# A decoder step on one core: first in-projection tiles ahead of the norm, tokens loaded in halves, the gate chain moved, and squares and splits interleaved at the key entry

## The chip, the cores and the metric

The kernel runs on one core of one Trainium2 chip. The metric is the device time of one execution in microseconds (us), as the median of several runs. PE is TensorE (matmuls), DVE is VectorE, ACT is ScalarE, POOL is GpSimd, and SP is the engine that here only issues transfers.

## The reference

One step of a small decoder with two layers, for 512 prompt tokens and 8 samples of 8 tokens each, together 576 token columns with 1024 features:

```
h = x
h += gdn_mixer(rmsnorm(h))        # h @ w_in -> causal conv of 4 taps -> silu -> q, k, v;
                                  # gates b, a -> beta, g; chunked gated delta rule; @ w_out
h += conv_ffn(rmsnorm(h))         # up, conv of 3 taps, silu, gate, down
k, v = rope(rmsnorm(h) @ w_kv)    # shared keys and values, computed once
h += diff_attention(rmsnorm(h), [paged cache, k], [paged cache, v])
h += conv_ffn(rmsnorm(h))
y = rmsnorm(h) * final_norm
```

All is float32. The outputs are y, the new recurrent state, the last rows before each convolution, and the new keys and values.

## The kernel before, in words

Features lie on the 128 partitions and tokens along the row: `hT` holds 8 blocks (m or k, 0 to 7) of 128 features by 576 tokens. A float32 product is made from three reduced-precision ones (`mm3`, L695): each operand is split into a high part (made by ACT: `high` for tokens, `weights` for weights) and a low part, the rest (made by DVE for tokens: `low`; by POOL for weights: its own `low`, or a line of its own in loops). The norm's factor per token is not multiplied into the tokens; it is multiplied into the product later (`rb`, a row of 576 factors; `rt`, the same by tokens), so products can begin before the norm is known.

The order of each engine's work is written out by hand: five programs run side by side and wait on semaphores. Loads go through SP's and ACT's queues.

**Entry.** PE turns the tokens from `X` into `hT` block by block (L680 to L686), with small transposes of the gains (L676) ahead and of the convolution rows (L691) in between. DVE evacuates a block (L1345) and makes the low part of the one before (L1347). ACT makes the high part and the squares of each block (L1921, L1922) and, before blocks 2 and 3, splits the two first weight tiles (L1919). POOL adds up the squares (L2346) and makes the low weights (L2345). Then PE computes the 16 gate columns (L806), the sums for the norm (L811), and the loop over the 32 in-projection tiles (`channels3`, L818 to L830). A tile is 128 output features: 48 matmuls of 288 columns (two token halves, eight blocks, three products). Two pairs of PSUM banks and two weight slots alternate, so tile t+2 waits for the evacuation of tile t and for the split of its weights.

**Tile loop.** For tiles 0 to 23 DVE multiplies by `rb` into a padded buffer (`pads`) and runs the four taps (L1396 to L1418). ACT then applies silu and, for the query and key tiles 0 to 15, squares the result (L1948 to L1955); PE adds these squares up with columns of one (`norm_sums`, ten short matmuls) one pair of tiles later. In ACT's program the split of the weights of tile t+2 stands ahead of the silu of tile t. Before DVE's tile loop stands the gate chain (L1352 to L1384): beta, decay and the attention's lambda, small operations that go back and forth between DVE and ACT.

**End of a feed-forward part.** The last eight tiles of the down-projection use four weight slots, so the last four refills are split while the tiles run. POOL makes the four low parts first (L2488), and then squares and adds the eight new blocks of `hT` (`square_sum`, L2495). In the first layer the low parts of the first two key tiles stand between the squares, at blocks 5 and 7 (L2494). DVE adds each tile to `hT` (L1621), makes the low tokens, and multiplies the gains into the first two key weight tiles after blocks 1 and 3 (`gain_in`, L1625). ACT makes the four high weights (L2141) and then the eight high token blocks (L2145). PE's key loop (L1080) begins when the first key tile's low weights are there. After the second layer the same sums feed the final norm (`norm(4, ...)`, L1286), and five token tiles are scaled by DVE and stored.

Of the kernel before, what the change touches and what calls it, by code (L numbers as in the profile page):

```python
# [22 lines left out]
P = 128  # L23
# [64 lines left out]
def yoco_step(nc, io):  # L88
# [7 lines left out]
    with ctx:  # L96
# [81 lines left out]
        lamv = at(O_R + 14000, 4, 64)  # L178
        lamt = at(O_R + 14256, 2, 64)
# [136 lines left out]
        ld_ss = sem("ld_ss")  # L316
        ld_kp = [sem(f"ld_kp{n}") for n in range(NPG)]
# [57 lines left out]
        def one_of(i, n=1):  # L375

            return slice(i * n, (i + 1) * n) if isinstance(i, int) else bass.ds(i * n, n)

# [75 lines left out]
        def _(sp):  # L454

            for s, n in ((cm_evac, 2), (siluA, 2), (tailA_done, 2), (up_act, 2), (up_tail, 2), (act_lo, 2), (dn_ev, 4), (d_o, 1),
                         (psc, 4), (pex, 4), (pam, 4), (pat, 4), (pae, 4), (ppv, 4), (poe, 4)):
                sp.sem_inc(s, n)
            with nc.allow_non_contiguous_dma(reason="small rows"):
                sp.dma_start(C[:, 0:C_PROMPT], consts[:, 0:C_PROMPT]).then_inc(ld_c, 16)  # L460
                sp.dma_start(X[:, 0:NT, :], x_prompt[0].rearrange("(t p) d -> p t d", p=P)).then_inc(ld_x, 16)
                sp.dma_start(X[0:ST, NT, :], x_sample.rearrange("s t d -> (s t) d")).then_inc(ld_x, 16)
                w_in = a_w_in[0].rearrange("(k p) n -> p k n", p=P)
                for n in range(2):
                    sp.dma_start(inW.raw[n], w_in[:, :, n * P:(n + 1) * P]).then_inc(ld_in[n], 16)
                sp.dma_start(C[:, C_PROMPT:C_END], consts[:, C_PROMPT:C_END]).then_inc(ld_pt, 16)
# [199 lines left out]
        def _(pe):  # L666
# [8 lines left out]
            pe.wait_ge(ld_g, 16 * 8)  # L675
            for m in range(KB):  # L676
                tr(PS[:, 0, 6 * m:6 * m + 6], rowsG[0:6, m * P:(m + 1) * P], 6)
            tr(PS[:, 0, 48:50], rowsH[0:2, 0:P], 2).then_inc(ct_done, 1)
            pe.wait_ge(ld_x, 32)
            for m in range(KB):  # L680
# [6 lines left out]
                if m < 2:  # L687
                    continue
                if m == 2:
                    pe.wait_ge(ld_ra, 32)  # L690
                for c in range(4 * (m - 2), 4 * (m - 1)):  # L691
                    last = tr(PS[:, 1 + c // 12, RA * (c % 12):RA * (c % 12 + 1)], rowsI[0:RA, c * P:(c + 1) * P], RA)
# [8 lines left out]
            def norm(n, bank, whole=True, tokens=None):  # L701
# [4 lines left out]
                if tokens is not None:  # L706
                    for t in range(NT):
                        mm(PS[:, tokens, t:t + 1], acc[:, t * P:(t + 1) * P], ones[:, 0:1])
                    mm(PS[0:ST, tokens, NT:NT + 1], acc[:, SEQ:T], ones[:, 0:1])
                    last = mm(PS[ST:P, tokens, NT:NT + 1], acc[:, SEQ:T], ones[:, 0:1])  # L710
# [92 lines left out]
            pe.wait_ge(h_ready, KB)  # L803
            pe.wait_ge(ct_evac, 2)
            pe.wait_ge(ab_x, 1)
            for h in range(2):  # L806
                for k in range(KB):
                    last = mm(PS[0:16, h, 0:HALF], wabg[:, k, :], hT[:, k, h * HALF:(h + 1) * HALF],
                              k == 0, k == KB - 1)
            last.then_inc(ab_mm, 1)  # L810
            norm(0, 4, True, 6)  # L811
# [4 lines left out]
            pe.wait_ge(xl_ready, X_A + 8)  # L816
            pe.wait_ge(ld_pt, 16 * 5)
            channels3(1, inW, W_IN, xh, xl, B_IN)  # L818
            channels3(H, inW, W_IN, xh, xl, B_IN, first=1, sums=True)
# [481 lines left out]
        def _(dve):  # L1301
# [18 lines left out]
            dve.wait_ge(ct_done, 1)  # L1320
            copy(gT.rearrange("p a b -> p (a b)"), PS[:, 0, 0:48]).then_inc(ct_evac, 1)
            link(copy(hgT, PS[:, 0, 48:50]))
            link(V.tensor_scalar(hgT[:, 1:2], hgT[:, 1:2], 1.0 - LAM_INIT, None, ALU.mult))
# [15 lines left out]
            dve.wait_ge(ld_sm, 16)  # L1339
            dve.wait_ge(ct_evac, 1)  # L1340
# [1267 lines left out]
```

## Time and profile before

| | |
|---|---|
| time, median of 3 runs | 2059.36 us (2058.04 to 2061.03) |
| profiled execution | 2059.37 us, its span 2057.7 us |
| PE busy | 1892.8 us (92%) |
| DVE busy | 1019.6 us (50%) |
| POOL busy | 888.6 us (43%) |
| ACT busy | 658.6 us (32%) |
| chain that ended last | PE 75%, DVE 8%, ACT 4%, POOL 4%, issue 4% |
| mean granted PE clock | 0.976 of full speed |

The span runs from the first to the last instruction; 1.7 us of the time lie around it. Busy time is an average over stages that have different limits, so the stages are read one by one.

### The profile page before, as it was taken

How to read it: one execution, taken by the hardware profiler on the slowest of the kernel's cores; microseconds unless marked ns; L12 is line 12 of the kernel's file. 1: busy time of each engine (PE TensorE's matmuls, PEld its weight loads, DVE VectorE, ACT ScalarE, POOL GpSimd, SP SyncE). 2: the span in 40 equal slices, each digit the busy share in tenths (PEclk: the TensorE clock that was granted, in tenths of full speed). 3: DMA queues.
4: the chain of work that ended last, by engine and by line, in shares of the span. 5: the costliest groups of instructions: out<-in, count | busy, mean ns of one | idle time of the engine just before them, and what ended most of it. 6: DMA issues, size and time to landing. Idle time of an engine off the chain costs nothing.

```text
span 2057.7 us, 36926 instructions
## 1 busy us (share of the span) xinstructions
PE 1892.8 (92%) x14094; PEld 1730.2 (84%) x14094; DVE 1019.6 (50%) x1627; ACT 658.6 (32%) x1101; POOL 888.6 (43%) x753
## 2 busy tenths in 40 slices
PE   6999968777888999999998999888989999999997
PEld 4999968776886999999997888555557999999997
DVE  3787635565445553352455623555553453353352
ACT  3553322333331432221222221344443332221221
POOL 3444533243054654564559232000005754464555
PEclk9999989998998999999999999999999999999998
DMA  4122310000055532222222231687782423222221
GB/s 125 52 71 72 82 38 21 1 0 0 0 134 139 144 90 83 82 82 82 82 61 82 85 118 58 222 299 250 273 287 69 121 84 89 84 82 82 82 61 50
DMA packets 244207, 201.59 MB, mean 98 GB/s; under 512 B 7541, under 2 KB 217719, under 8 KB 243873
## 3 DMA queue, kind: packets, MB, share of 16 engines
q1 hardware_dynamic: 234948, 170.48, 27.6%
q10 hardware_dynamic: 9164, 29.80, 4.0%
q8 instruction: 65, 1.06, 0.2%
q14 instruction: 30, 0.25, 0.0%
HBM read 187.72 MB, written 12.53 MB: 97 GB/s over the span
## 4 chain that ended last, share of the span: by engine, by line
PE 75%; DVE 8%; ACT 4%; POOL 4%; issue 4%; ACTq 2%; DMA 1%; SPq 0%; DVEq 0%; POOLq 0%
PE PS L668 72%; PE PS L671 4%; DVE f L1310 4%; ACT f L1868 2%; POOL f L2309 2%; DVE f L1413 1%; DVE f L1307 1%; POOL f L2325 1%; ACT f L1871 1%; ACTq L2218 1%; POOL r L2319 1%; ACTq L2216 1%; DMA f<-in_cache_k 1%; DMA f<-in_a_w_in 1%; DVE r L1330 1%
## 5 line engine op out<-in xcount | busy, mean ns | idle before, releaser
L668 PE MATMUL PS<-r,r 128*128 128x288 f32 (+2 forms) x9168 | 1315.1, 305 | 20.9 <-POOL r L2319 13.3
L668 PEld LDWEIGHTS PS<-r,r 128*128 128x128 f32 x9168 | 1263.2, 189 | 54.7 <-POOL r L2319 13.2
L1310 DVE TENSOR_TENSOR f<-PS,f 128x512 f32<-128x512 f32 (+10 forms) x463 | 227.5, 517 | 532.4 <-PE PS L668 504.3
L2464 POOL TENSOR_TENSOR r<-f,r 128x1024 fp32r<-128x1024 f32 x128 | 312.4, 2444 | 303.6 <-ACT r L1871 303.6
L1871 ACT ACTIVATE r<-f 128x1024 fp32r<-128x1024 f32 (+5 forms) x263 | 259.2, 997 | 468.4 <-PE PS L668 380.9
L668 PE MATMUL PS<-f,f 128*32 128x256 f32 (+14 forms) x2124 | 239.7, 379 | 43.6 <-POOL f L2309 12.9
L2309 POOL TENSOR_TENSOR f<-f,f 128x512 f32<-128x512 f32 (+1 forms) x155 | 145.3, 956 | 230.1 <-DVE f L1310 151.4
L1871 ACT ACTIVATE f<-PS 128x512 f32<-128x512 f32 (+3 forms) x230 | 124.7, 560 | 374.1 <-PE PS L671 200.0
L668 PEld LDWEIGHTS PS<-f,f 128*32 128x32 f32 (+4 forms) x2124 | 145.8, 146 | 106.4 <-issue 66.3
L671 PE MATMUL PS<-f,f 128*128 128x128 f32 (+5 forms) x1226 | 175.7, 286 | 58.9 <-DVE f L1310 21.0
L668 PE MATMUL PS<-f 128*128 128x128 f32 x1504 | 193.0, 287 | 33.8 <-ACT f L1871 23.2
L671 PEld LDWEIGHTS PS<-f,f 128*128 128x128 f32 (+5 forms) x1226 | 139.8, 146 | 97.5 <-issue 51.5
L668 PEld LDWEIGHTS PS<-f 128*128 128x128 f32 x1504 | 184.8, 201 | 40.1 <-ACT f L1871 23.4
L2319 POOL TENSOR_TENSOR r<-f,r 128x1024 fp32r<-128x1024 f32 (+1 forms) x44 | 134.2, 3055 | 194.4 <-ACT r L1871 193.2
L2309 POOL TENSOR_TENSOR f<-f 128x1 f32<-128x1 f32 (+4 forms) x140 | 105.4, 753 | 256.3 <-PE PS L668 195.9
L1868 ACT ACTIVATE f<-f 128x512 f32 (+7 forms) x230 | 109.7, 500 | 275.1 <-DVE f L1655 179.3
L1307 DVE COPY f<-PS 128x512 f32<-128x512 f32 (+7 forms) x179 | 106.7, 600 | 176.5 <-PE PS L671 99.3
L1310 DVE TENSOR_TENSOR f<-f,f 128x1 f32<-128x1 f32 (+6 forms) x99 | 97.1, 981 | 62.6 <-DMA f<-in_w_kv 28.7
L1655 DVE SCALAR_TENSOR_TENSOR f<-f,f,f 128x592 f32<-128x592 f32 x88 | 116.5, 1324 | 3.1
L1310 DVE TENSOR_TENSOR f<-f,PS 128x64 f32<-128x64 f32 (+2 forms) x148 | 53.9, 414 | 110.6 <-POOL f L2309 108.7
L2353 POOL TENSOR_TENSOR r<-f,r 128x1024 fp32r<-128x1024 f32 x24 | 60.0, 2500 | 104.4 <-ACT r L1871 104.4
L1413 DVE SCALAR_TENSOR_TENSOR f<-f,f,f 128x600 f32<-128x600 f32 x72 | 103.6, 1439 | 2.5
(74 smaller groups left out, 699.7 us busy)
## 6 DMA issues: line engine op xcount, KB each, us to landing
f<-in_f_w_up SPq DMA_DIRECT2D x88, 512.0 KB, 4.0
f<-in_cache_k SPq DMA_DIRECT2D x64, 512.0 KB, 4.7
f<-in_cache_v ACTq DMA_DIRECT2D x56, 512.0 KB, 6.6
f<-in_a_w_in SPq DMA_DIRECT2D x32, 512.0 KB, 4.1
f<-in_f_w_down SPq DMA_DIRECT2D x32, 512.0 KB, 4.0
f<-in_a_w_out SPq DMA_DIRECT2D x16, 512.0 KB, 4.2
f<-in_w_kv SPq DMA_DIRECT2D x8, 1024.0 KB, 5.2
out<-f SPq DMA_DIRECT2D x13, 512.0 KB, 4.8
```

Source lines behind the costliest of these rows:

```text
L668: return nc.tensor.matmul(out, lhsT, rhs, start=start, stop=stop)
L671: return nc.tensor.transpose(out, in_, ident[0:n, 0:n])
L1307: return V.tensor_copy(out, in_)
L1310: return V.tensor_tensor(out, a, b, op)
L1413: ins = V.scalar_tensor_tensor(cv[:, 0:m], pad[:, a:a + m], tp[:, w + a:w + a + 1], cv[:, 0:m], ALU.mult, ALU.add)
L1655: ins = V.scalar_tensor_tensor(cv[:, 0:m], pad[:, a:a + m], tp[:, w + a:w + a + 1], cv[:, 0:m], ALU.mult, ALU.add)
L1868: return A.activation(out, in_, func, **kw)
L1871: return A.activation(out, in_, ACT.Copy)
L2309: return G_.tensor_tensor(out, a, b, ALU.mult)
L2319: G_.tensor_tensor(w.lo2[n], w.raw2[n], w.hi_f[n], ALU.subtract).then_inc(w_lo, 1)
L2353: G_.tensor_tensor(inW.lo2[n], inW.raw2[n], inW.hi_f[n], ALU.subtract).then_inc(w_lo, 1)
L2464: G_.tensor_tensor(upW.lo2[n], upW.raw2[n], upW.hi_f[n], ALU.subtract).then_inc(w_lo, 1)
```

## The change

At the entry, SP starts its transfers before it sets its initial semaphore counts, and loads the tokens as two halves of 512 features. PE turns blocks 0 and 1 before the gains, and the convolution rows in blocks 4 to 7, six at a time, into banks 2 and 7. In-projection tile 0 is computed block by block as the low tokens appear, then tile 1, then the norm's sums, then the gate columns. ACT takes a copy of a constant early. On DVE and ACT the tile pairs 0 and 1 run before the gate chain; the last two steps of lambda are moved behind the tile loop.

At the key entry, ACT's `high` of blocks 0 to 2 stands between the last refills, DVE's `gain_in` stands after blocks 2 and 5, and POOL's squares stand between its refills, in both layers; the low parts of the key tiles come at blocks 4 and 6.

```diff
@@ SP @@
-            for s, n in ((cm_evac, 2), (siluA, 2), ...
-                sp.sem_inc(s, n)
...
-                sp.dma_start(X[:, 0:NT, :], x_prompt[0].rearrange("(t p) d -> p t d", p=P)).then_inc(ld_x, 16)
-                sp.dma_start(X[0:ST, NT, :], x_sample.rearrange("s t d -> (s t) d")).then_inc(ld_x, 16)
+                for half, landed in ((slice(0, D // 2), ld_x), (slice(D // 2, D), ld_x2)):
+                    sp.dma_start(X[:, 0:NT, half], x_prompt[0, :, half].rearrange("(t p) d -> p t d", p=P)
+                                 ).then_inc(landed, 16)
+                    sp.dma_start(X[0:ST, NT, half], x_sample[:, :, half].rearrange("s t d -> (s t) d")
+                                 ).then_inc(landed, 16)
...
@@ PE @@
-            pe.wait_ge(h_ready, KB)
+            def in_tile(n, f, ks):
+                c = slice(f * HALF, (f + 1) * HALF)
+                for k in ks:
+                    if n == 0 and f == 0:
+                        pe.wait_ge(xl_ready, X_A + k + 1)
+                    last = mm3(PS[:, 2 * n + f, 0:HALF], inW.hi[n][:, k, :], inW.lo[n][:, k, :],
+                               xh[:, k, c], xl[:, k, c], k == 0, k == KB - 1)
+                return last
+
+            pe.wait_ge(w_lo, W_IN + 1)
+            for ks in (range(5), range(5, KB)):
+                for f in range(2):
+                    last = in_tile(0, f, ks)
+            last.then_inc(cm_done, 1)
+            pe.wait_ge(w_lo, W_IN + 2)
             pe.wait_ge(ct_evac, 2)
+            for f in range(2):
+                last = in_tile(1, f, range(KB))
+            last.then_inc(cm_done, 1)
+            norm(0, 4, True, 5, 400)
...
-            norm(0, 4, True, 6)
+            channels3(2, inW, W_IN, xh, xl, B_IN, first=1, sums=True)
             pe.wait_ge(ab_ev, 1)
...
-            channels3(1, inW, W_IN, xh, xl, B_IN)
-            channels3(H, inW, W_IN, xh, xl, B_IN, first=1, sums=True)
+            channels3(H, inW, W_IN, xh, xl, B_IN, first=2, sums=True)
...
@@ DVE @@
+            dve.wait_ge(rb_ready, 1)
+            conv_pair(0)
+            conv_pair(1)
             dve.wait_ge(ld_pt, 16 * 5)
             dve.wait_ge(ab_mm, 2)
...
-            with dve.Fori(0, NQ // 2) as i:
+            with dve.Fori(2, NQ // 2) as i:
+                ch.enter(10 * i + (-20))
+                conv_pair(i)
...
-                    if xbase == X_KV and m in (1, 3):
-                        gain_in(m // 2)
+                    if xbase == X_KV and m in (2, 5):
+                        gain_in(m // 3)
@@ ACT @@
+            act.wait_ge(eps_set, 1)
+            copy(tock, eps)
             act.wait_ge(ct_evac, 1)
...
+            key_pair(0, 0)
+            key_pair(1)
             act.wait_ge(ab_x, 2)
...
+            act.wait_ge(cm_done, 5)
+            act.wait_ge(ld_in[0], 16 * 4)
+            weights(inW, 0)
             f(sp2, sp2, ACT.Ln, bias=one).then_inc(ab_exp, 1)
...
+            key_pair(2, 1)
+            with act.Fori(3, H) as i:
+                key_pair(i)
...
                     for m in range(KB if p < 2 else 4):
                         refill(m // 4, m % 4, TB[p] + 2 * NB[p])
+                        if l == 0 and p == 2 and m:
+                            act.wait_ge(cm_evac, B_DN[l] + m + 2)
+                            high(m - 1, None)
                 if l == 0:
-                    for m in range(KB):
+                    for m in range(3, KB):
@@ POOL @@
-                    for m in range(KB if p < 2 else 4):
-                        refill(m // 4, m % 4, TB[p] + 2 * NB[p])
-                    if p == 2:
-                        for m in range(KB):
-                            if l == 0 and m in (5, 7):
-                                pool.wait_ge(ft_done, FT - 2 if m == 5 else FT)
+                    for m in range(KB):
+                        if p < 2 or m < 4:
+                            refill(m // 4, m % 4, TB[p] + 2 * NB[p])
+                        if p == 2:
+                            if l == 0 and m in (4, 6):
+                                pool.wait_ge(ft_done, FT - 2 if m == 4 else FT)
                                 low(kvW, m // 2 - 2, W_KV + m // 2 - 2)
                             square_sum(m, B_DN[l] + 3 + m, slice(0, T))
```

The new `conv_pair` and `key_pair` are the loop bodies of before as functions; `key_pair(i, refill)` splits weights only for the last `refill` tiles of its pair, because the splits of the first two pairs' successors now stand at other places.

On PE, at the entry, before (`f_5120_112` are the tokens in `X`, `f_3072_115` the convolution rows, `f_4608_50` is `hT`, `f_576_53` the sum of squares, `r_5120` the split tokens):

```order
L671 MATMUL PS<-f_2706_56,f_5120_112 128x128 x4
L671 MATMUL PS<-f_2706_56,f_5120_112 128x64
L671 MATMUL PS<-f_2706_56,f_3072_115 128x28 x4
L668 MATMUL PS<-f_4608_50,f_128_117 16x288 x16
L668 MATMUL PS<-f_576_53,f_2706_56 128x288 x2
L668 MATMUL PS<-f_2706_56,f_576_53 128x1 x4
L668 MATMUL PS<-f_2706_56,f_576_53 64x1 x2
L671 MATMUL PS<-f_2706_56,f_640_118 128x16 x5
L715 UNCONDITIONAL_BRANCH
L668 MATMUL PS<-r_5120_51,r_1024_106 128x288
```

The same place on PE now, from the end of tile 1 on (the two tiles ahead of it are 96 rows like the first one):

```order
L677 MATMUL PS<-r_5120_51,r_1024_109 128x288
L677 MATMUL PS<-f_576_53,f_2706_56 128x288 x2
L677 MATMUL PS<-f_2706_56,f_576_53 128x1 x4
L677 MATMUL PS<-f_2706_56,f_576_53 64x1 x2
L677 MATMUL PS<-f_4608_50,f_128_117 16x288 x16
L729 UNCONDITIONAL_BRANCH
L677 MATMUL PS<-r_5120_51,r_1024_106 128x288
```

The gate columns (16x288) stood between the transposes and the first tile; they now stand behind tile 1 and the norm's sums.

On POOL, at the end of the first feed-forward part, before (`r_1024` are low down-projection weights, `f_576_54` a block's squares, `r_2048` the low key weights):

```order
L2464 TENSOR_TENSOR r_1024_109<-f_1024_104,r_1024_107 128x1024
L2464 TENSOR_TENSOR r_1024_150<-f_1024_105,r_1024_147 128x1024
L2464 TENSOR_TENSOR r_1024_151<-f_1024_145,r_1024_148 128x1024
L2464 TENSOR_TENSOR r_1024_152<-f_1024_146,r_1024_149 128x1024
L2309 TENSOR_TENSOR f_576_54<-f_4608_50 128x576
L2325 TENSOR_TENSOR f_576_53<-f_576_53,f_576_54 128x576
```

The same place on POOL now:

```order
L2518 TENSOR_TENSOR r_1024_109<-f_1024_104,r_1024_107 128x1024
L2363 TENSOR_TENSOR f_576_54<-f_4608_50 128x576
L2379 TENSOR_TENSOR f_576_53<-f_576_53,f_576_54 128x576
L2518 TENSOR_TENSOR r_1024_150<-f_1024_105,r_1024_147 128x1024
L2363 TENSOR_TENSOR f_576_54<-f_4608_50 128x576
L2379 TENSOR_TENSOR f_576_53<-f_576_53,f_576_54 128x576
L2518 TENSOR_TENSOR r_1024_151<-f_1024_145,r_1024_148 128x1024
L2363 TENSOR_TENSOR f_576_54<-f_4608_50 128x576
L2379 TENSOR_TENSOR f_576_53<-f_576_53,f_576_54 128x576
L2518 TENSOR_TENSOR r_1024_152<-f_1024_146,r_1024_149 128x1024
L2363 TENSOR_TENSOR f_576_54<-f_4608_50 128x576
L2379 TENSOR_TENSOR f_576_53<-f_576_53,f_576_54 128x576
```

A square and an addition now stand behind each of the four splits; in the first layer the first key split follows four of the eight squares instead of five.

## Rows read from the trace of the kernel before

**Rows 1.** Timeline of PE, entry: start, length (us), operation, count, [idle before <- releaser].

```profile
34.32 13.00 PE L668 MATMUL PS<-f,f 128*16 128x288 f32 x48 [6.54 <-issue]
...
47.66 12.93 PE L668 MATMUL PS<-r,r 128*128 128x288 f32 x96
...
72.07 9.18 PE L668 MATMUL PS<-r,r 128*128 128x288 f32 x48 [2.22 <-POOL r L2353]
...
82.12 6.58 PE L668 MATMUL PS<-r,r 128*128 128x288 f32 x48
...
119.37 6.58 PE L668 MATMUL PS<-r,r 128*128 128x288 f32 x48
```

**Rows 2.** Windows: stretch, length, PE busy, granted clock, DMA share, GB/s.

```profile
72.00:74.00 2.00, 1.93 (x8) 0.50 0.23 38
```

**Rows 3.** Timeline, key entry, of POOL and PE.

```profile
1078.74 4.73 POOL L2464 TENSOR_TENSOR r<-f,r 128x1024 fp32r<-128x1024 f32 x2 [5.57 <-ACT r L1871]
...
1096.49 1.55 POOL L2309 TENSOR_TENSOR f<-f 128x576 f32<-128x576 f32 x1
...
1100.03 3.08 POOL L2309 TENSOR_TENSOR f<-f 128x576 f32<-128x576 f32 x1
...
1112.09 4.56 POOL L2319 TENSOR_TENSOR r<-f,r 128x2048 fp32r<-128x2048 f32 x1
...
1116.70 16.77 PE L668 MATMUL PS<-r,r 128*128 128x512 f32 x60 [9.94 <-POOL r L2319]
...
1134.40 8.55 PE L668 MATMUL PS<-r,r 128*128 128x512 f32 x36
```

**Rows 4.** Timeline, final norm, of DVE, POOL and PE.

```profile
2034.02 0.76 DVE L1310 TENSOR_TENSOR f<-PS,f 128x576 f32<-128x576 f32 x1 [3.98 <-PE PS L668]
...
2037.58 1.15 POOL L2309 TENSOR_TENSOR f<-f 128x576 f32<-128x576 f32 x1
2038.80 1.39 POOL L2325 TENSOR_TENSOR f<-f,f 128x576 f32<-128x576 f32 x1
...
2040.30 2.07 PE L668 MATMUL PS<-f,f 128*128 128x1 f32 x12 [3.50 <-POOLq L2496]
```

**Rows 5.** Timeline of SP's queue: issue of the first two weight tiles.

```profile
3.17 1.46 SPq L465 DMA_DIRECT2D f<-in_a_w_in  x2
```

**Rows 6.** Transfers issued from 3.1 to 3.7 us: count, size, us to landing.

```profile
f<-in_a_w_in SPq DMA_DIRECT2D x1, 512.0 KB, 14.7
```

**Rows 7.** Timeline, entry, of ACT, POOL and DVE.

```profile
19.24 1.04 ACT L1871 ACTIVATE r<-f 128x1024 fp32r<-128x1024 f32 x1
...
29.04 8.61 POOL L2346 TENSOR_TENSOR f<-f,f 128x576 f32<-128x576 f32 x5
...
33.37 0.84 DVE L1307 COPY f<-PS 128x672 f32<-128x672 f32 x1
...
45.19 0.74 ACT L1871 ACTIVATE f<-PS 16x576 f32<-16x576 f32 x2 [13.44 <-PE PS L668]
...
47.36 1.04 ACT L1868 ACTIVATE f<-PS,f 128x5 f32<-128x5 f32 x2
...
50.77 0.44 DVE L1310 TENSOR_TENSOR f<-PS,f 128x40 f32<-128x40 f32 x2 [16.56 <-ACT f L1868]
```

**Rows 8.** Timeline, tile loop, of DVE and ACT.

```profile
57.83 0.18 DVE L1307 COPY f<-f 128x28 f32 x1
...
62.55 2.61 DVE L1413 SCALAR_TENSOR_TENSOR f<-f,f,f 128x600 f32<-128x600 f32 x3
...
65.28 1.28 ACT L1868 ACT_TABLE_LOAD   x1 [5.52 <-DVE f L1413]
...
97.92 4.62 DVE L1413 SCALAR_TENSOR_TENSOR f<-f,f,f 128x600 f32<-128x600 f32 x3
```

**Rows 9.** Timeline, key weights, of DVE.

```profile
1122.34 6.46 DVE L1310 TENSOR_TENSOR f<-f,f 128x2048 f32<-128x2048 f32 x1 [10.04 <-DMA f<-in_w_kv]
...
1159.00 2.29 DVE L1310 TENSOR_TENSOR f<-f,f 128x2048 f32<-128x2048 f32 x1 [5.92 <-DMA f<-in_w_kv]
```

More of the change, by code:

```diff
@@ L316, in yoco_step @@
         ld_ss = sem("ld_ss")
+        ld_x2 = sem("ld_x2")
         ld_kp = [sem(f"ld_kp{n}") for n in range(NPG)]
@@ L699, in mm3, with norm @@
                 return mm(out, wl, h, False, stop)
-            def norm(n, bank, whole=True, tokens=None):
+            def norm(n, bank, whole=True, tokens=None, col=0):
                 pe.wait_ge(acc_ready, n + 1)
@@ L1871, in copy, with norm @@
                 return A.activation(out, in_, ACT.Copy)
-            def norm(n, bank, whole=True, tokens=None):
+            def norm(n, bank, whole=True, tokens=None, col=0):
                 act.wait_ge(nrm_mm, n + 1)
@@ L1878, in norm @@
                 if tokens is not None:
-                    link(f(rt, PS[:, tokens, 0:NT + 1], ACT.Ln, bias=eps, scale=1.0 / D))
+                    link(f(rt, PS[:, tokens, col:col + NT + 1], ACT.Ln, bias=eps, scale=1.0 / D))
                 if whole:
@@ L1922, in _, with silu_block, key_pair @@
                 f(sqb[k], hT[:, k, :], ACT.Square).then_inc(sq_ready, 1)
-            act.wait_ge(ab_mm, 1)
-            copy(two(abT[0:16, 0:T]), PS[0:16, 0:2, 0:HALF])
-            copy(abT[0:16, T:TD], PS[0:16, 1, HALF - ST:HALF]).then_inc(ab_ev, 1)
-            norm(0, 4, True, 6)
+            for n in range(2):
+                act.wait_ge(cm_done, n + 1)
+                act.wait_ge(ld_in[n], 32)
+                weights(inW, n)
+            norm(0, 4, True, 5, 400)
+            act.wait_ge(ab_mm, 1)
+            copy(two(abT[0:16, 0:T]), PS[0:16, 6:8, 0:HALF])
+            copy(abT[0:16, T:TD], PS[0:16, 7, HALF - ST:HALF]).then_inc(ab_ev, 1)
+            def silu_block(i, n, refill=True):
+                if refill:
+                    act.wait_ge(cm_done, 2 * i + (n + 1))
+                    act.wait_ge(ld_in[n], 16 * i + 32)
+                    weights(inW, n)
+                act.wait_ge(convA, 2 * i + (n + 3))
+                blk = qkvT[:, block_of(2 * i + n), :].rearrange("p a b -> p (a b)")
+                f(blk[:, 0:SEQ], cvA[n][:, 0:SEQ], ACT.Silu)
+                f(blk[:, SEQ:T].rearrange("p (s x) -> p s x", s=NS),
+                  cvA[n][:, SEQ + CA - 1:LA].rearrange("p (s x) -> p s x", s=NS)[:, :, 0:TS],
+                  ACT.Silu).then_inc(siluA, 1)
+                return blk
+            def key_pair(i, refill=2):
+                for n in range(2):
+                    blk = silu_block(i, n, n >= 2 - refill)
+                    act.wait_ge(siluA, 2 * i + (n + 3))
+                    act.wait_ge(sq_used, 2 * i + (KB + n - 1))
+                    copy(tock, eps)
+                    f(sqn[n][:, 0:SEQ], blk[:, 0:SEQ], ACT.Square)
+                    f(sqh[n][:, n * ST:(n + 1) * ST], blk[:, SEQ:T], ACT.Square).then_inc(sq_ready, 1)
+            key_pair(0, 0)
+            key_pair(1)
             act.wait_ge(ab_x, 2)
@@ L1966, in _ @@
                     f(nrm, nrm, ACT.Exp, scale=-0.5).then_inc(ab_exp, 1)
+                    act.wait_ge(lam_v, 1)
+                    f(lame, lams, ACT.Exp).then_inc(lam_e, 1)
                 if m < H - 2:
```

151 lines of the change are left out of this document (69 added, 82 removed).

## The prediction

> **What bounds the kernel now.** The chain that ended last is PE for three quarters, so time can only be won where PE idles while others work. I read PE's timeline for idle stretches ahead of its rows, then looked up in the other engines' timelines what ended each. The change touches three.
>
> The first is the entry. PE begins its first projection tile at 47.66 us, after 13 us of gate columns and norm sums that were themselves held back to 34.32 [rows 1]. Tiles 2 and 3 then come late: tile 3 waits 2.22 us and takes 9.18 us instead of 6.58 [rows 1], with the clock at half, the 1.2 GHz level [rows 2]. Only from tile 4 at 82.12 on does PE run without a break: the tile that starts at 119.37 is the fifth after it, so a tile with its sums takes 37.25/5 = 7.45 us [rows 1]. In that loop PE is the bound, and what tile 4 gains the loop hands on.
>
> The second is the key entry: PE ends the down-projection at 1116.70 - 9.94 = 1106.76 and idles until POOL has made the first low key weights [rows 3]. The third is the final norm, where PE idles 3.50 us behind POOL's last square [rows 4].
>
> **The entry.** The tokens in halves win little by themselves. ACT must split the first weight tile before token block 2, and these weights land at 3.17 + 14.7 = 17.9 us, behind the tokens [rows 5, 6]. Before, ACT reached that split at 19.24 [rows 7]; now it waits for the weights. SP's earlier start and the shorter rows of the halves (no row shows them) pull in opposite directions, so I keep 17.9, give or take 1.5. All behind this split keeps its order on ACT, DVE and POOL: 1.3 us are won there, and the last low tokens, done at 33.4 just ahead of the 33.37 row [rows 7], come at 32.1. ACT's early copy moves a table load, the gains move behind block 1, the convolution rows to blocks 4 to 7; all of this lies in the wait for the weights and costs nothing, but none of it wins anything either while the weights are late.
>
> Now PE has done five blocks of tile 0 by then; 12 matmuls of 12.93/96 = 0.135 us remain, so tile 0 ends at 33.7 and tile 1, 6.5 us, at 40.2. The sums for the norm need POOL's additions, which ended at 37.65 and end 1.3 earlier [rows 7]: no wait. The 13.0 us row splits at the gate columns' release of ACT, 45.19 [rows 1, 7]: columns 10.8, sums 2.2. Sums first gives 42.4; ACT and its two table loads need 50.77 - 47.36 = 3.4 us [rows 7]; `rb` is there at 45.8. PE spends 42.4 to 53.2 on the gate columns, while DVE already convolves.
>
> DVE's tile: an estimated 2.0 us of evacuation and small steps (what the 65.28 - 57.83 = 7.45 us of the first tile leave, less a first tap that POOL held up) and three tap operations, which take 2.61 us alone and 4.62 beside POOL [rows 8]: 4.6 to 6.6 us. Tiles 0 and 1 end at 45.8 + 6.6 + 4.6 = 57.0. PE does tile 2 from 53.2 to 59.6 and tile 3 from 60.7 to 67.1, each with 1.1 us of sums behind it. DVE ends tile 2 at 66.2 and tile 3 at 67.1 + 6.6 = 73.7. Then comes the gate chain, 57.83 - 50.77 = 7.1 us of DVE and ACT in turn [rows 7, 8]. Its added wait: ACT still has tile 3's silu and squares and one weight split to do, some 2.5 us more, and behind DVE's waiting instruction stands the evacuation of tile 4, for which PE's tile 6 waits. DVE reaches tile 4 at 83.3, PE's tile 6 runs from 84.2 to 90.6, its sums to 91.7. Tile 7 is the next late one: its weights are split behind tile 4's squares. DVE ends tile 4 between 87.9 and 89.9; from a convolution's end to the next tile's start lay 72.07 - 65.28 = 6.8 us, 1.28 of them a table load that now stands earlier [rows 1, 8], so 5.5: tile 7 starts between 93.4 and 95.4. Before it started at 82.12 + 3 x 7.45 = 104.5. That wins 9.1 to 11.1; I take 9.5, nearer to the contended end, as DVE runs beside POOL in the loop. From here DVE's 6.6 us per tile are below PE's 7.45, so PE closes up and carries the 9.5 on. The value tiles behind are paced by DVE in both kernels and shift with it. The last two lambda steps, two small DVE operations, now stand behind the loop while PE turns the convolution tails: nothing.
>
> **The key entry.** POOL's work up to the first low key weights begins with its first split at 1078.74, 4.73/2 = 2.4 us each [rows 3]. It was four splits, five squares and the key split of 4.56; now it is four splits, four squares and the key split, without the gaps in which POOL waited for ACT. A square with its addition takes 1100.03 - 1096.49 = 3.5 us beside DVE [rows 3] and 2.7 alone (1.15 + 1.39 and the gaps) [rows 4]. So the weights are ready at 1078.74 + 9.5 + 4 x 2.7 + 4.6 = 1103.6 at best and 1106.8 at worst, which is just when PE is free. The 9.9 us of idle time go. The sixty matmuls behind it took 16.77 us where the next 36 took 8.55 [rows 3]; at that rate they take 14.25, which returns another 2.5. What is late next: the norm sums behind them. PE is there at 1106.8 + 14.25 = 1121.1; POOL has two more squares, the second key split and two squares to do, and is done between 1119.4 and 1125.8; I take 1122.5, a wait of 1.4. Sum: 9.9 + 2.5 - 1.4 = 11.0, with 7.6 to 12.4 as ends. Refills held behind squares: the fourth ends at 1096.0 to 1099.0, and PE needs it for the last tile only, 4.8 us before 1106.8, at 1102.0. DVE's additions wait behind `gain_in`, which now stands later, so PE's banks come free in time. The key loop behind is PE's own, and the shift stays.
>
> At one place the order of POOL and DVE is disputed. DVE's product on a key weight tile took 2.29 us alone and 6.46 beside POOL [rows 9]. The Trainium skill (SBUF — State Buffer, Who interferes with whom) says that a DVE instruction with two SBUF inputs and a GpSimd instruction that reads SBUF exclude each other for the whole instruction. These rows agree; by that rule the squares, now moved beside DVE's low parts, would not merely slow but queue, which is the second rival below. By it the sum would be 16.4 us, by mere slowing the 24.1 below.
>
> **The final norm.** The last block is in `hT` at 2034.02 + 0.76 = 2034.8 [rows 4], and POOL, having squared the others meanwhile, needs 2.7 us: 2037.5, where it was 2040.2. PE's sums then stand 0.7 us behind its transposes instead of 3.5, and their 2.07 us are those of a slow clock after the idle stretch [rows 4]; at full clock I count 0.9 less. Sum 3.6, ends 2.7 and 4.
>
> **The sum.** 9.5 + 11.0 + 3.6 = 24.1 us off the profiled execution's 2059.37 (2057.7 of span and 1.7 around it; its time is the median of the runs): 2035.3 us. A difference under 0.2%, some 4 us, cannot be told from none.
>
> **Rivals.** First: the entry gains less. For it speaks that tile 7 still waits some 2 to 4 us after the sums, as tile 3 did before it ran at half clock; such a fall costs 9.18 - 6.58 = 2.6 [rows 1]. Weights that land 1.5 us later cost as much again. Against it: at the uncontended end the wait is 93.4 - 91.7 = 1.7 us, less than the 2.22 ahead of the slow tile. If the gate chain's stall eats all of it, the time is 2044.8; with the fall and the late weights 2039.4. I give 2040.
>
> Second: at the key entry POOL and DVE queue instead of sharing. Five low tokens, each like the 0.76 us of an addition of their shape [rows 4], and two products of 2.29 [rows 9] stand beside POOL there, 8.4 us; added to the uncontended 1103.6 that makes 1112.0, so PE idles 5.2, and a slow first stretch returns: 7.7 us lost, 2043. Against it: the measured contended squares already hold such waits.
>
> Third, slower: the lag of the tile loop never closes. Each tile's weights are split behind the squares of an earlier tile, and if DVE's tile beside POOL took over 7.45 us, each key tile would be like tile 3: 82.12 - 72.07 = 10.05 us [rows 1], 2.6 over the loop's. Over 14 tiles that is 36 us, and with 24.1 won elsewhere the time is 2072. It decides from ten tiles on. Against it speaks DVE's 6.6.
>
> Fourth: the change does not do what it says, since tile 0 waits for the same weights, POOL's order hides behind ACT's, and only the final norm is won: 2056.
>
> **How the numbers follow.** The forecast, 2029 to 2041, has 0.53. The first rival has 0.20, the second 0.18, the third 0.05, the fourth 0.04. The range goes from all the favourable ends (entry 13 with weights landing 1.5 us early, key entry 12.4, norm 4: 2030) to the first two rivals together (2048): 2030 to 2048. Faster: 0.53 + 0.20 + 0.18 and a third of the fourth, 0.92; same 0.03; slower 0.05.
>
> **What would show it.** In the profile after: tile 0's matmuls start near 21 us and are broken by waits until 32; the row of 16-column gate matmuls begins near 42; tile 7 starts near 95 and the 7.45 us pace holds from there. At the key entry POOL's rows alternate between splits and squares and the sixty matmuls follow the last down tile without a gap and take about 14.3 us. At the end POOL's last addition ends 2.7 us after DVE's last one. The prediction is wrong if the first weights land after 20 us, if PE still waits at tiles 8 and 9, or if the sixty matmuls still wait more than 3 us for POOL.

## The result, and the profile after

The changed kernel takes 2048.97 us (median of five, 2043.47 to 2051.28) against 2059.36 for the kernel before: ratio 0.9948, 95% interval 0.9929 to 0.9967. The forecast was 2035.3 with a range of 2030 to 2048. The direction was right; 10.4 us were won where 24.1 were forecast.

The profiled execution is the fastest of the five (2043.47 us, span 2041.7). I read PE's timeline first, at the three places of the prediction. The entry (columns as in [rows 1]):

```profile
26.35 14.36 PE L677 MATMUL PS<-r,r 128*128 128x288 f32 x96
40.55 9.99 PE L677 MATMUL PS<-f,f 128*128 128x288 f32 x48
50.48 6.62 PE L677 MATMUL PS<-r,r 128*128 128x288 f32 x48
...
82.41 6.58 PE L677 MATMUL PS<-r,r 128*128 128x288 f32 x48 [1.48 <-DVE f L1340]
...
90.87 6.60 PE L677 MATMUL PS<-r,r 128*128 128x288 f32 x48 [0.87 <-POOL r L2407]
...
98.34 6.58 PE L677 MATMUL PS<-r,r 128*128 128x288 f32 x48
```

Tiles 0 and 1 now stand ahead of the gate columns; tiles 6 and 7 wait 1.5 and 0.9 us; from tile 7, at 90.87, the pace is 7.45 us. Against [rows 1] tile 7 is 13.6 us earlier.

The key entry, PE:

```profile
1097.41 14.07 PE L677 MATMUL PS<-r,r 128*128 128x512 f32 x60 [1.38 <-POOL r L2373]
1120.09 2.17 PE L677 MATMUL PS<-f,f 128*128 128x1 f32 x12 [8.61 <-POOLq L2550]
1122.19 9.92 PE L677 MATMUL PS<-r,r 128*128 128x512 f32 x36
```

The 9.94 us of [rows 3] are gone from the sixty matmuls, and 8.61 us stand one step further on, ahead of the norm sums: PE waits for POOL's last addition. The granted clock falls in that wait, so the 36 matmuls that took 8.55 us in [rows 3] take 9.92:

```profile
1116.00:1120.00 4.00, 0.00 (x0) 0.00 (x0) 2.73 (x1) 0.00 (x0) 3.91 (x2) 0.50 0.00 0
```

(Stretch, length, PE, weight loads, DVE, ACT, POOL busy, granted clock, DMA share, GB/s.) A clock of 0.50 is the 1.2 GHz level; only DVE and POOL work. The final norm, DVE's last addition, POOL's square and sum, and PE:

```profile
2022.41 0.76 DVE L1340 TENSOR_TENSOR f<-PS,f 128x576 f32<-128x576 f32 x1 [3.99 <-PE PS L677]
...
2023.31 1.15 POOL L2363 TENSOR_TENSOR f<-f 128x576 f32<-128x576 f32 x1 [0.51 <-DVE f L1340]
2024.54 1.40 POOL L2379 TENSOR_TENSOR f<-f,f 128x576 f32<-128x576 f32 x1
...
2026.04 1.27 PE L677 MATMUL PS<-f,f 128*128 128x1 f32 x12 [0.85 <-POOLq L2550]
```

Here POOL is no longer behind: the square follows DVE's addition, and PE waits 0.85 us where [rows 4] had 3.50.

### The profile page after: what moved, and what is told of

Its sections match the earlier page's. It is cut to its first block, busy times and chain, and to the rows that moved or that the text cites. A ratio compares the mean times of both kernels' runs of the same rounds, so it can differ in the third digit from the quotient of the medians.

```text
span 2041.7 us, 36838 instructions
## 1 busy us (share of the span) xinstructions
PE 1888.5 (92%) x14094; PEld 1729.5 (85%) x14094; DVE 1021.0 (50%) x1627; ACT 640.1 (31%) x1088; POOL 899.6 (44%) x753
## 4 chain that ended last, share of the span: by engine, by line
PE 74%; DVE 8%; ACT 4%; POOL 4%; issue 3%; ACTq 1%; DMA 1%; SPq 0%; DVEq 0%; POOLq 0%
PE PS L677 71%; PE PS L680 4%; DVE f L1340 3%; ACT f L1905 2%; DVE f L1410 2%; POOL f L2363 1%; ACT f L1908 1%; POOL r L2373 1%; DVE f L1337 1%; POOL f L2379 1%; ACTq L2272 1%; DMA f<-in_cache_k 1%; ACTq L2270 1%; ACT L1905 1%; POOL r L2518 0%
## 5 line engine op out<-in xcount | busy, mean ns | idle before, releaser
L1340 DVE TENSOR_TENSOR f<-PS,f 128x512 f32<-128x512 f32 (+9 forms) x463 | 227.3, 516 | 516.5 <-PE PS L677 504.8
L680 PE MATMUL PS<-f,f 128*128 128x128 f32 (+4 forms) x1226 | 173.5, 284 | 57.0 <-DVE f L1340 20.2
L680 PEld LDWEIGHTS PS<-f,f 128*128 128x128 f32 (+4 forms) x1226 | 138.7, 146 | 95.5 <-issue 50.8
L1905 ACT ACTIVATE f<-f 128x64 f32 (+9 forms) x230 | 109.5, 500 | 312.3 <-DVE f L1692 179.2
```

Of the source, the lines that this page charges most:

```text
L680: return nc.tensor.transpose(out, in_, ident[0:n, 0:n])
L1340: return V.tensor_tensor(out, a, b, op)
L1905: return A.activation(out, in_, func, **kw)
```

## Experiments

All 15 runs are edits of the changed kernel, except before_again and final_alone, which are edits of the kernel before. Each ratio is to the kernel before on the same chip, whose median was between 2059.5 and 2063.5 us there.

**Two executions that can be compared.** again and before_again repeat both kernels with nothing edited, for a second profile of each.

> The changed kernel once more, with nothing edited. Its first five times spread from 2043.5 to 2051.3 us and its profile is of the fastest. Theory: the others lost their time in stretches at the lower clock, so the median is again 2047 to 2051, and if this profile is of a slower execution its tile 7 still starts within 1 us of 90.9, PE still waits 8 to 9 us ahead of the kv norm sums, and what it is behind the first profile appears in stretches with a granted clock under 1. Rival: the spread comes from waits at the entry that fall differently; then tile 7 moves by several microseconds with the time.

> The kernel before once more, for a second profile. In the changed kernel, one profile runs the first FFN tile (27 matmuls behind 2.17 us of idle) at the full clock in 3.86 us and another in 6.53 us at a granted clock near 0.57, and one of the stretch near 600 us differs likewise by 1.6 us. Theory: these falls come and go between executions of either kernel, so a profile of the kernel before may show them too (its first profile, 3.85 us, did not), and its time then lies 2 to 5 us above 2058. Rival: only the change brings them (by shifting all that follows by 10 to 13 us); then this profile again shows 3.85 us and no fall near 600 us.

Measured: again 2047.64 us, ratio 0.9928 (0.9905 to 0.995), its profile 2048.21; before_again 2058.89, one execution. PE in before_again:

```profile
72.68 6.60 PE L668 MATMUL PS<-r,r 128*128 128x288 f32 x48 [2.21 <-POOL r L2353]
...
117.40 6.58 PE L668 MATMUL PS<-r,r 128*128 128x288 f32 x48
...
185.35 89.68 PE L668 MATMUL PS<-r,r 128*128 128x288 f32 x672
...
689.13 5.18 PE L668 MATMUL PS<-r,r 128*128 128x288 f32 x27 [2.16 <-DVE r L1330]
...
1117.02 16.46 PE L668 MATMUL PS<-r,r 128*128 128x512 f32 x60 [9.93 <-POOL r L2319]
...
1143.42 0.66 PE L671 MATMUL PS<-f,f 128*128 128x128 f32 x4 [0.47 <-DVE f L1310]
...
2039.84 1.68 PE L668 MATMUL PS<-f,f 128*128 128x1 f32 x12 [3.54 <-POOLq L2496]
```

and in again:

```profile
83.74 7.89 PE L677 MATMUL PS<-r,r 128*128 128x288 f32 x48 [1.49 <-DVE f L1340]
...
107.39 6.58 PE L677 MATMUL PS<-r,r 128*128 128x288 f32 x48
...
175.34 90.91 PE L677 MATMUL PS<-r,r 128*128 128x288 f32 x672
...
681.35 6.53 PE L677 MATMUL PS<-r,r 128*128 128x288 f32 x27 [2.17 <-DVE r L1356]
...
1101.99 14.14 PE L677 MATMUL PS<-r,r 128*128 128x512 f32 x60 [1.35 <-POOL r L2373]
1124.64 2.17 PE L677 MATMUL PS<-f,f 128*128 128x1 f32 x12 [8.51 <-POOLq L2550]
1126.74 10.57 PE L677 MATMUL PS<-r,r 128*128 128x512 f32 x36
1137.15 0.60 PE L680 MATMUL PS<-f,f 128*128 128x128 f32 x4
...
2030.47 1.26 PE L677 MATMUL PS<-f,f 128*128 128x1 f32 x12 [0.85 <-POOLq L2550]
```

The long waits are the same in both executions of a kernel; the lengths of the rows behind them are not. The 27 matmuls of the first FFN tile stand behind 2.17 us of idle each time and take 3.86 us in the first profile of the change and 6.53 here, at this clock (columns as above):

```profile
680.00:684.00 4.00, 2.65 (x11) 2.65 (x12) 1.96 (x4) 0.00 (x0) 4.00 (x3) 0.57 0.43 128
684.00:688.00 4.00, 4.00 (x20) 3.95 (x20) 0.00 (x0) 0.00 (x0) 1.84 (x1) 0.58 0.61 175
```

The kernel before shows such a fall there too (5.18 us), so the rival, that only the change brings them, falls, though its time, 2058.89, is not the 2 to 5 us above 2058 that were expected with a fall; and its tile 3 ran at full speed this time (6.60 us, 9.18 in [rows 1]). The other rival, that waits at the entry move the spread, has a small part: in again the wait ahead of tile 6 also let the clock fall, 7.89 us for 6.58. The runs below show which picture is the usual one. Of ten profiles with the entry of the change (all but the four with the gate edit, below), nine show a fall at tile 6 or 7, of 7.85 to 8.16 us; only the first does not. The first FFN tile took 5.4 to 6.6 us in 13 of 14. In the three profiles with the entry of before (before, before_again, final_alone) tile 3 took 9.18, 6.60 and 9.17 us, the first FFN tile 3.85, 5.18 and 6.62. So the first profile of the change is the exception at both places.

The pair again and before_again, taken on two chips, lies 10.7 us apart, close to the 10.4 of the result's medians; it serves for the accounts. How far again stands ahead of before_again:

| place | ahead by, us |
|---|---|
| tile 9 of the tile loop, 117.40 to 107.39 | 10.0 |
| end of the value tiles' row (275.0 to 266.3) | 8.8 |
| start of the first FFN tile, 689.13 to 681.35 | 7.8 |
| last down tile's end, 1117.02 - 9.93 to 1101.99 - 1.35 | 6.5 |
| first transposes of the keys, 1143.42 to 1137.15 | 6.3 |
| span, 2057.3 to 2046.4 | 10.9 |

**The parts one by one.** entry_alone puts both FFNs' last stretch back; key_back that of the first alone; final_alone takes only that of the second; tokens_whole undoes the halves. The edit of POOL's loop in key_back (with the gains back at m 1 and 3, POOL's key splits at 5 and 7, and ACT's high parts behind its refills):

```diff
-                    for m in range(KB):
-                        if p < 2 or m < 4:
+                    late = l == 0 and p == 2
+                    for m in range(4 if late else 0):
+                        refill(m // 4, m % 4, TB[p] + 2 * NB[p])
+                    for m in range(KB):
+                        if not late and (p < 2 or m < 4):
```

> The changed kernel with both FFNs' last stretch as before, so that of the change the entry alone is left. Theory: entry and final norm add up, the key entry is worth nothing: the final norm alone won 4 to 5 us of a before of 2060 and the changed kernel 11 to 13, so this wins 7 to 9 (2051 to 2054), and in its profile the tile loop's steady pace stands 10 us ahead of that of the kernel before where neither ran a tile at the lower clock. Rival: the entry's lead is eaten by the stages behind it: under 4 us, 2056 or more.

> The changed kernel with the key entry as it was before (POOL's four refill splits ahead of its squares, gains behind the 2nd and 4th addition, ACT's high parts behind all its refills); entry and final norm keep the change. Theory: the key entry as a whole is worth under 1 us, since PE now waits 8.6 us for the norm sums in place of 9.9 us for the key weights: time within 2 us of the changed kernel's 2049, and the sixty matmuls again start about 10 us behind the last down tile. Rival: the key entry does give most of its forecast 11 us, and the missing time is lost elsewhere: 2057 to 2060.

> The kernel before with the interleaved squares and splits in the second FFN alone. Theory: the final norm gains what it was forecast to, 2.7 to 4.4 us: the last square starts when the last addition ends, PE waits 0.8 us instead of 3.5, and the time is 2055 to 2057 beside a before of 2059 to 2061. Then entry and clock falls make up the rest of the changed kernel's 10 to 14 us. Rival: POOL's squares, moved among its splits, hold a refill up there and the gain is under 1 us.

Measured: entry_alone 2051.38 us, ratio 0.9963 (0.9949 to 0.9977), by the ratio 7.6 us; final_alone 2055.53, ratio 0.9976 (0.9962 to 0.9989), 4.9 us; key_back 2047.52, ratio 0.9936 (0.9913 to 0.996), against again's 2047.64 on the same chip. So entry and final norm, 12.5 us together, make up the change (10.4 us in the result, 14.8 by again's ratio), and the key entry is worth nothing that these times can show. key_back's PE has the old picture back and arrives no later:

```profile
1110.80 15.82 PE L677 MATMUL PS<-r,r 128*128 128x512 f32 x60 [9.94 <-POOL r L2370]
...
1127.55 8.55 PE L677 MATMUL PS<-r,r 128*128 128x512 f32 x36
```

Its 36 matmuls end at 1136.1 (1127.55 + 8.55), again's at 1137.3.

```diff
-                for half, landed in ((slice(0, D // 2), ld_x), (slice(D // 2, D), ld_x2)):
-                    ...
+                sp.dma_start(X[:, 0:NT, :], x_prompt[0].rearrange(...)).then_inc(ld_x, 16)
+                sp.dma_start(X[0:ST, NT, :], x_sample.rearrange(...)).then_inc(ld_x, 16)
```

> The changed kernel with the tokens loaded whole, by one transfer of the prompt and one of the samples, as before; all else as changed. Theory: the first weights, which land at about 17.2 us, set the entry, and the halves win under 1.3 us: tile 7 starts between 90.5 and 92.5 us and the time is within 1.5 us of the changed kernel's 2048. Rival: the halves carry the entry: with whole tokens the first transposes start 2 to 4 us later, ACT reaches the weights only behind them, and tile 7 and the time come 3 to 4 us later (2051 to 2052).

Measured: 2048.03 us, ratio 0.994 (0.9921 to 0.9958). PE's first transposes and ACT's first weight split:

```profile
11.29 12.90 PE L676 MATMUL PS<-f,f 128*128 128x128 f32 x62 [11.29 <-DMA f<-in_x_sample]
...
17.83 1.04 ACT L1902 ACTIVATE r<-f 128x1024 fp32r<-128x1024 f32 x1
```

The transposes start 2.8 us later than again's 8.47, yet the split stands at 17.83 against 17.64. In again ACT waits 2.54 us for the weights there; with whole tokens it comes to the split without a wait. So the weights set the entry of the changed kernel, and the halves win nothing that can be measured.

**What PE waits for at the key entry.** Three edits: DVE's third and fourth gain behind POOL's last addition (gain_later), POOL's second key split there (key_order), six of the eight squares on ACT (act_squares).

```diff
 gain_later (DVE)
+            dve.wait_ge(acc_ready, 3)
             for q in (2, 3):
                 gain_in(q)
 key_order (POOL)
-                            if l == 0 and m in (4, 6):
+                            if l == 0 and m == 4:
...
             ffn(0)
+            pool.wait_ge(ft_done, FT)
+            low(kvW, 1, W_KV + 1)
 act_squares (ACT, POOL)
                         high(m, None)
+                        f(sqk[m - 2], hT[:, m, :], ACT.Square).then_inc(ksq, 1)
...
+                            if l == 0 and m >= 2:
+                                pool.wait_ge(ksq, m - 1)
+                                link(G_.tensor_tensor(acc, acc, sqk[m - 2], ALU.add))
```

> DVE's third and fourth gain products wait for POOL's last norm addition, and so stand behind POOL's squares and splits and not beside them. Theory: a DVE product on a key weight tile and POOL's instructions exclude each other, each such product costs POOL its own 2.3 us: POOL's last addition ends 4 to 4.6 us earlier against the last down tile, the wait ahead of the norm sums falls from 8.6 to about 4.4, and the time from 2049 to 2045. Rival A: POOL's instructions are slow by themselves: its rows, the wait and the time stay (2049). Rival B: the gains are now late for ACT's next weights: PE waits behind the norm sums instead, 2049 or more.

> The changed kernel with POOL's second key split behind its last two squares. Theory: the sum of POOL's work bounds the key entry, not its order: the norm sums come some 6 us earlier (PE's wait ahead of them falls from 8.6 to 2 to 3 us) but PE then waits 3 to 5 us for the second key split, and only the 2 us of the sums themselves and their slow clock are hidden: 2 to 4 us off the changed kernel's 2048, 2044 to 2046. Rival: only the order was wrong: both waits go and it gains 9 to 11 us, 2037 to 2039.

> At the key entry ACT squares token blocks 2 to 7 (six activations of 0.67 us) and POOL only adds them. Theory: what bounds the key entry is the sum of POOL's work, 52 us from its first refill split to its last addition without a gap; without six multiplications of 1.2 to 3.2 us it is some 36 to 40 us, POOL is done before the sixty matmuls end, and both waits (1.4 and 8.6 us) and the slow matmuls behind them (some 2.4 us) go: 2049 - 12 = 2037, 2035 to 2040. Rival: ACT's added 4 us hold up its key weight halves, so that POOL's second key split stays late and PE waits 3 to 5 us there: 2041 to 2045.

gain_later took 2046.95 us, ratio 0.9923 (0.9901 to 0.9944). First DVE and POOL in the changed kernel, behind the first key split:

```profile
1106.17 6.71 DVE L1340 TENSOR_TENSOR f<-f,f 128x2048 f32<-128x2048 f32 x1
...
1106.04 4.69 POOL L2373 TENSOR_TENSOR r<-f,r 128x2048 fp32r<-128x2048 f32 x1
1110.70 3.19 POOL L2363 TENSOR_TENSOR f<-f 128x576 f32<-128x576 f32 x1
1113.97 1.39 POOL L2379 TENSOR_TENSOR f<-f,f 128x576 f32<-128x576 f32 x1
1115.44 1.15 POOL L2363 TENSOR_TENSOR f<-f 128x576 f32<-128x576 f32 x1
1116.66 3.32 POOL L2379 TENSOR_TENSOR f<-f,f 128x576 f32<-128x576 f32 x1
```

then the same last four POOL rows and PE's wait in gain_later:

```profile
1117.22 1.14 POOL L2364 TENSOR_TENSOR f<-f 128x576 f32<-128x576 f32 x1
1118.44 1.39 POOL L2380 TENSOR_TENSOR f<-f,f 128x576 f32<-128x576 f32 x1
1119.92 1.15 POOL L2364 TENSOR_TENSOR f<-f 128x576 f32<-128x576 f32 x1
1121.14 1.40 POOL L2380 TENSOR_TENSOR f<-f,f 128x576 f32<-128x576 f32 x1
...
1122.64 2.17 PE L677 MATMUL PS<-f,f 128*128 128x1 f32 x12 [4.63 <-POOLq L2551]
```

The two rows that took 3.19 and 3.32 take 1.14 and 1.40; the wait falls from 8.6 to 4.63, as expected. The changed kernel's DVE product, 2.29 us alone [rows 9], lasts until 2.2 us behind POOL's split (1110.73 to 1112.88), and POOL's next multiplication lasts 1.0 beyond it: they take turns. The stage, from the last down tile's end to the first transposes of the keys, takes 32.8 us, in again 36.5. The time fell by 0.7 us against again, within the scatter, where 4 were expected; so the gain is shown in the stage, not in the median.

key_order took 2045.63 us, ratio 0.9932 (0.9916 to 0.9948):

```profile
1117.93 1.27 PE L677 MATMUL PS<-f,f 128*128 128x1 f32 x12 [1.92 <-POOLq L2550]
1122.63 10.87 PE L677 MATMUL PS<-r,r 128*128 128x512 f32 x36 [3.44 <-POOL r L2373]
```

One wait of 8.5 became two of 1.92 and 3.44, and PE still waits for the end of POOL's work: another order moves the wait. The stage takes 32.8 us here too: the norm's sums now run beside POOL's split, and POOL's work is 1.8 us shorter (50.1 us from the first split, 51.9 in again), since the fourth gain now falls behind it. The sum of POOL's work is the bound, not its order. The median does not tell this version from again (ratio 0.9928).

act_squares took 2038.21 us, ratio 0.988 (0.9859 to 0.9901), 9.4 us below again on the same chip, and within the 2035 to 2040 expected. PE, POOL's last additions and DVE's last low token:

```profile
1113.07 3.02 PE L679 MATMUL PS<-r,r 128*128 128x512 f32 x12 [0.88 <-DVE r L1339]
1115.92 1.16 PE L679 MATMUL PS<-f,f 128*128 128x1 f32 x12
1117.01 8.59 PE L679 MATMUL PS<-r,r 128*128 128x512 f32 x36
...
1110.70 3.28 POOL L2556 TENSOR_TENSOR f<-f,f 128x576 f32<-128x576 f32 x2
...
1106.55 4.81 DVE L1342 TENSOR_TENSOR r<-f,r 128x576 fp32r<-128x576 f32 x1 [0.77 <-ACT r L1910]
```

POOL is done at 1114, 1.9 us before PE asks. No wait for POOL is left and the 36 matmuls run at the full clock. What is left is 0.88 us for DVE, whose low token took 4.81 us beside POOL's second key split.

**Versions that go further.** best and best_gate add to act_squares the late split and six squares on ACT in the second FFN; sq_final and sq_final_gate leave the split at its place. The gate edit, by itself in gate_split and gate_again, convolves a pair of tiles inside the gate chain:

```diff
             V.scalar_tensor_tensor(sp2, sp1, -1.0, sp1, ALU.mult, ALU.max).then_inc(ab_x, 1)
+            conv_pair(2)
             dve.wait_ge(ab_exp, 1)
...
-            with dve.Fori(2, NQ // 2) as i:
+            with dve.Fori(3, NQ // 2) as i:
```

> In the changed kernel DVE convolves tiles 4 and 5 between the first and the second part of the gate chain, and so does not stand 5.7 us waiting for ACT's exponentials. Theory: the two waits left in PE's entry (1.48 us ahead of tile 6, 0.87 us ahead of tile 7) come from this stall; they go, tile 7 starts 2 to 2.4 us earlier, near 88.5, and the time falls by as much, 2045.5. Rival: DVE's work in the tile loop is the bound there and not the stall, or ACT's own chain takes the stall's place: tile 7 moves by less than 0.5 us and the time stays at 2048.

> The kernel with six squares on ACT, with two edits more: POOL's second key split behind its last addition (there it no longer stands beside DVE's last low token, which took 4.81 us, and PE waited 0.88 us for it), and six squares on ACT in the second FFN too (0.67 us on ACT in place of POOL's 1.15 behind the last addition). Theory: 0.9 + 0.5 us less than the 2038.2 of the six squares, 2036 to 2038. Rival: the second key split, now later, is what PE waits for behind the norm sums: 2039 to 2042.

> The kernel of the run before this one, and in addition tiles 4 and 5 convolved between the parts of the gate chain. In the changed kernel this took both waits away (tile 7 at 88.9 us in place of 90.9 to 92.5), but its median time did not fall. Theory A: the 2 us are real and were covered by stretches at the lower clock that vary from one execution to the next: 2 us below the run before this one, with tile 7 again near 88.9. Theory B: what is won at the entry is given back by falls of the clock behind it, in this kernel too: no difference within 1 us, and the profile shows one more slow stretch.

> Six squares on ACT in both FFNs, POOL's second key split back at its place beside the squares. Theory: what cost the last version 6 us at the key entry (PE idle 5.35 us behind DVE) was the late split: the next key weights are loaded only behind it, DVE's fourth gain waits for them, and PE's first transposes wait for DVE. With the split earlier this goes, and the time is that of the six squares in the first FFN, 2038.2, less 0.9 at the final norm: 2036 to 2039. Rival: the wait was POOL's or ACT's own; it stays, 2043 to 2045.

> The kernel of the run before this one with tiles 4 and 5 convolved between the parts of the gate chain. Theory: 2 us at least, and up to 5 where the wait that goes had also let the clock fall: 2031 to 2036, below the run before this one on the same chip. Rival: no difference within 1 us.

> The changed kernel with tiles 4 and 5 convolved between the parts of the gate chain, for a second profile: its first execution took 2043.4, its others 2047.9 to 2051.4. Theory: tile 7 again starts near 88.9 us, and what this execution is behind the first stands in stretches at a granted clock under 1 in the stages behind the entry. Rival: the waits ahead of tiles 6 and 7 come back in some executions.

best took 2044.07 us, ratio 0.9928 (0.9914 to 0.9941), by the ratios slower than act_squares, where 2036 to 2038 were expected:

```profile
1104.06 1.16 DVE L1342 TENSOR_TENSOR r<-f,r 128x576 fp32r<-128x576 f32 x1 [0.77 <-ACT r L1910]
...
1118.28 6.60 DVE L1342 TENSOR_TENSOR f<-f,f 128x2048 f32<-128x2048 f32 x3 [9.50 <-DMA f<-in_w_kv]
...
1127.29 1.12 PE L682 MATMUL PS<-f,f 128*128 128x128 f32 x4 [5.35 <-DVE f L1342]
```

The low token now takes 1.16, but the next key weights are loaded only behind the split, DVE's fourth gain waits 9.50 us for them, and PE 5.35 for DVE. sq_final, with the split back, took 2036.51 us, ratio 0.9874 (0.9846 to 0.9903), and PE's wait there is 0.47 us, which confirms the cause in the stage. It need not be all of best's loss: best_gate has the same wait, 5.36 us, and took 2037.82.

The gate edit does what it says: tile 7 starts at 88.87 in gate_split and between 88.4 and 89.4 in all four profiles with it, without a wait and without a fall of the clock. Its worth in time is not settled; the 2 us or more that were expected are not borne out, since the three pairs on one chip disagree: gate_split is 1.4 us slower than tokens_whole, best_gate 6.3 faster than best, sq_final_gate 1.2 faster than sq_final. gate_split took 2049.47 (ratio 0.9947, 0.9929 to 0.9965) beside tokens_whole's 2048.03; gate_again 2043.33, one execution; best_gate 2037.82 (0.9898, 0.9881 to 0.9915) against best's 2044.07; sq_final_gate 2035.31 (0.9872, 0.9843 to 0.9901; 2026.67 to 2038.02) against sq_final's 2036.51. sq_final and sq_final_gate beat both kernels: by their ratios 1.3% below the one before, where the changed kernel stood 0.5 to 0.7% below it.

## Why the prediction was wrong

None of the three signs of being wrong that the prediction named came: ACT had the weights at 17.24 us, PE did not wait at tiles 8 and 9, and the sixty matmuls waited 1.38 us. The prediction watched the wait that it removed; the loss stood one step behind it.

**The entry: right in its direction, too low, and close to the pair's figure by luck.** The forecast of 9.5 counted from [rows 1], whose tile 3 ran at the lower clock; in that count tile 7 came 13.6 us earlier. Where no tile ran at the lower clock in either kernel it is 11.6 (tile 9, 117.40 in before_again, 105.78 in the first profile after). The pair's 10.0 includes again's slow tile 6. ACT reached the weights at 17.24 (17.9 forecast), the last low tokens were done at 31.8 (32.1), `rb` came at 46.4 (45.8). Tile 0 started at 26.35, behind all transposes, and not near 21, which cost little: tile 1 ended at 40.6 (40.2). The gate columns with the sums took 9.99 us where the sum carried 13.0 over from [rows 1] (why they are shorter is not shown), so tile 2 started at 50.5 and not at 53.2, and tile 7 came 2.5 us or more ahead of its forecast. That the halves win little by themselves was right. The first rival's fall of the clock did come in nine of ten profiles, at 1.3 to 1.6 us and not 2.6; its smaller gain at the entry did not.

**The key entry: wrong, and most of the miss.** Forecast 11.0, measured -0.2 (the lead goes from 6.5 to 6.3): 11.2 of the 13.2 us that the pair falls short of 24.1. The 9.9 us ahead of the sixty matmuls went as forecast but for 1.35, and they took 14.1 (14.25). The step that failed is the next one: "POOL has two more squares, the second key split and two squares to do, and is done between 1119.4 and 1125.8; I take 1122.5, a wait of 1.4." In the same count (again's last addition ends at 1124.5, and its lead is 6.5) POOL was done at 1131.0 and PE waited 8.5. The term that was mis-sized is POOL's work from its first split to its last addition: 43.8 us were taken (1122.5 - 1078.74), 52.0 measured. (The step's own terms give 1119.0 and 1125.4 for its ends; the 0.4 us change nothing.) POOL's first split in the first profile of the change, and its last addition in the kernel before:

```profile
1068.00 2.40 POOL L2518 TENSOR_TENSOR r<-f,r 128x1024 fp32r<-128x1024 f32 x1 [5.57 <-ACT r L1908]
```

```profile
1129.88 1.43 POOL L2325 TENSOR_TENSOR f<-f,f 128x576 f32<-128x576 f32 x1
```

From 1068.00 to 1119.98 (1116.66 + 3.32, above) POOL has no gap, so a moved square returns one step later, and the sum is what counts. The kernel before had 52.6 us, from the 1078.74 of [rows 3] to 1131.31, with 3.1 us of gaps inside: the gaps went, as forecast, but the work grew by 2.5. For a square beside DVE was sized from one row of [rows 3] at 3.5 us, while the four that took turns with a gain lasted 4.5 to 5.1; [rows 3] show that dearer kind too, in the 3.08 us of the multiplication at 1100.03, beside which a gain ran from 1098.58 to 1102.10. The gains now all lie within POOL's span; the fourth stood behind it before, at 1131.73.

That is the second rival's mechanism, at another place than it named: the weights were late by 1.4 us and not 5.2, the norm sums by 8.5. Its rule is that of the Trainium skill (SBUF — State Buffer, Who interferes with whom): a DVE instruction with two SBUF inputs contends with a GpSimd instruction that reads SBUF, and contention there is an exclusive lock. gain_later agrees: two gains of 2.29 us out of the way gave POOL 4.0 us back, twice 2.0.

**The final norm: right.** Forecast 3.6; 4.2 between the pair of profiles (10.9 at the end, 6.7 ahead of it), 4.9 (2.3 to 7.8) by final_alone's ratio. The fall of PE's wait is 2.7 us, as forecast. The sums' own clock gave 0.4 in the pair where 0.9 were counted, and 1.1 us more came behind the sums, which no term covers; so the 4.2 stand a little above the forecast's upper end of 4.

**What the sum had no term for.** Between entry and key entry the lead goes from 10.0 to 6.5 us. In the pair 1.2 of this is the value tiles' row (90.91 against 89.68) and 1.35 the first FFN tile (6.53 against 5.18); in again the clock was 0.91 at the start of the value tiles, where before_again had 1.00, and 0.57 at the FFN tile. The other 1.0 lies between these two, in steps of about half a microsecond. The first profile of before had no fall at the FFN tile and one at tile 3, so the entry could show a gain that the rest of an execution did not keep. Whether the change makes these falls likelier behind the entry is open: the value tiles' row is slow in two of the three profiles with the entry of before as well (91.0 and 92.4 us), against eight of the ten with the change and without the gate edit, and three are too few to say.

The third and fourth rivals are out: the 7.45 us pace holds from tile 7, and entry_alone wins 7.6 us.

## What to carry to other kernels

When a wait for a busy engine is removed by reordering that engine's work, add up all its work until the last thing anyone needs from it: if it has no gaps, the wait reappears at the next thing that is late, and only what shortens that sum (here squares moved to ACT, or gains moved out of POOL's way) shortens the stage. Where the trace shows the two taking turns, as here, put every two-input product of DVE that falls into POOL's span into POOL's sum at nearly its own length (2.0 of 2.29 us). And compare two profiles of each kernel before booking a slow row as a gain.

## What was not expected of the hardware

Behind the same wait of 2.17 us the first FFN tile ran at the full clock in two of 17 profiles and at a lower one in the others, down to 0.57: 3.86 and 6.53 us for the same 27 matmuls, 5.18 in between. A wait of 1.49 us ahead of tile 6 did it too in some, 7.89 for 6.58, and not in others. And a late instruction on POOL cost most through a transfer: in best the split itself made nobody wait, the load behind it did, by 5.35 us at PE.
